# Token tiles of a hybrid encoder's projection placed as runs of rows inside the levels of a delta-rule scan

## The reference

```
proj = x @ w_in                                   # (256, 1024) x (1024, P_IN)
pg, pr, pm = split(proj)
# gMLP: u, v = gelu(pg); v = norm(v) * g + b; y = ws @ v (positions of a chunk of 128) + bs; out = u * y
# RWKV-7, 6 heads x 64, two directions, per step:
sa = state @ a; state = state * w + outer(sa, b) + outer(v, k); out_t = state @ r
# matrix memory (mLSTM), 6 heads x 64, two directions, chunks of 128:
#   gates = pm's last 24 columns -> sums, maxima; scores q k^T weighted by exp(...); num / den; head norm; sigmoid(o)
mix = concat(groups) @ w_out
x = layer_norm(alpha * x + mix)
x = layer_norm(alpha * x + top4_of_32_experts(x))
```

## Time and profile before

| | |
|---|---|
| runs | 1183.06, 1183.63, 1185.85 us, median 1183.63 |
| the profiled execution | span 1184.3 us; the page gives it no other time |
| PE busy | 1132.2 us (96%), 5708 matmuls |
| DVE, ACT, POOL busy | 284.8, 221.9, 33.7 us |
| granted TensorE clock | 0.997 on the mean |
| DMA | 430.95 MB, queue 1 busy 86.2% |
| chain that ended last | PE 73%, DMA 21%, ACT 3%, DVE 2% |

### The profile page before, as it was taken

The page is one execution under the profiler, slowest core; times in us unless marked ns, Lnnn a source line. Parts: engine busy times, 40 slices in busy tenths (PEclk is TensorE's granted clock), DMA queues, the critical chain, the costliest instruction groups (busy, mean ns, idle before and its releaser), DMA issues.

```text
span 1184.3 us, 14440 instructions
## 1 busy us (share of the span) xinstructions
PE 1132.2 (96%) x5708; PEld 493.9 (42%) x5708; DVE 284.8 (24%) x738; ACT 221.9 (19%) x519; POOL 33.7 (3%) x70
## 2 busy tenths in 40 slices
PE   7999999999999999999999999999999999999997
PEld 6875778753333333333333333333333333333332
DVE  1368666662111111111111111111111111111112
ACT  1245655412111111111111111111111111111102
POOL 1000222100000000000000000000000000000000
PEclk9999999999999999999999999999999999999999
DMA  8525202599999999999999999999999999999995
GB/s 336 196 81 198 108 1 78 195 343 390 428 427 429 427 427 428 427 428 428 429 428 427 429 428 429 428 428 429 429 429 428 428 429 429 428 428 428 429 423 217
DMA packets 35649, 430.95 MB, mean 364 GB/s; under 512 B 4086, under 2 KB 4262, under 8 KB 8860
## 3 DMA queue, kind: packets, MB, share of 16 engines
q1 hardware_dynamic: 34364, 428.27, 86.2%
q0 software_dynamic: 528, 1.02, 0.3%
q10 hardware_dynamic: 720, 1.15, 0.3%
HBM read 429.37 MB, written 1.06 MB: 363 GB/s over the span
## 4 chain that ended last, share of the span: by engine, by line
PE 73%; DMA 21%; ACT 3%; DVE 2%; issue 1%; POOLq 0%; SPq 0%; POOL 0%; ACTq 0%; DVEq 0%
PE bank L1484 25%; PE bank L1503 16%; DMA ring<-in_exp_w 14%; DMA pool<-in_exp_w 7%; PE bank L1063 5%; PE bank L1456 4%; PE bank L1440 4%; PE bank L1073 3%; PE bank L1363 2%; PE bank L1468 2%; PE bank L1535 2%; ACT pool L967 1%; PE bank L1238 1%; PE bank L1253 1%; PE bank L1245 1%; PE bank L1528 1%
## 5 line engine op out<-in xcount | busy, mean ns | idle before, releaser
L1484 PE MATMUL bank<-ring,pool 128*64 128x512 f32 x1200 | 265.4, 593 | 10.9 <-DMA ring<-in_exp_w 10.9
L1484 PE MATMUL bank<-pool 128*64 128x512 f32 x848 | 188.4, 594 | 7.1 <-DMA pool<-in_exp_w 7.1
L1484 PEld LDWEIGHTS bank<-ring,pool 128*64 128x64 f32 x1200 | 85.2, 137 | 186.5 <-issue 162.4
L1503 PE MATMUL bank<-ring,pool 128*64 128x512 f32 x620 | 137.7, 595 | 3.8 <-ACT pool L967 3.8
L2191 DVE TENSOR_SCALAR pool<-pool 128x128 f32<-128x128 f32 x64 | 19.4, 346 | 474.1 <-PE bank L1484 474.1
L1484 PEld LDWEIGHTS bank<-pool 128*64 128x64 f32 x848 | 59.9, 137 | 130.6 <-issue 115.2
L942 ACT ACTIVATE pool<-pool 128x512 f32<-128x512 f32 x32 | 20.2, 631 | 416.8 <-DVE pool L2203 416.8
L1503 PE MATMUL bank<-pool 128*64 128x512 f32 x404 | 90.1, 595 | 2.7 <-ACT pool L967 2.7
L2203 DVE TENSOR_SCALAR pool<-bank 128x512 f32<-128x512 f32 x32 | 22.2, 693 | 258.1 <-PE bank L1484 258.1
L1503 PEld LDWEIGHTS bank<-ring,pool 128*64 128x64 f32 x620 | 42.9, 137 | 85.0 <-issue 77.6
L1063 PE MATMUL bank<-pool,ring 128*128 128x256 f32 x272 | 62.1, 391 | 7.0 <-DMA ring<-in_w_in_C 7.0
(11 more groups left out here) (311 smaller groups left out, 903.1 us busy)
## 6 DMA issues: line engine op xcount, KB each, us to landing
ring<-in_exp_w SPq DMA_DIRECT2D x110, 2048.0 KB, 31.9
pool<-in_exp_w SPq DMA_DIRECT2D x73, 2048.0 KB, 34.7
pool<-in_exp_w SPq DMA_DIRECT2D x9, 1024.0 KB, 8.1
ring<-in_exp_w SPq DMA_DIRECT2D x6, 1024.0 KB, 38.4
ring<-in_w_out SPq DMA_DIRECT2D x2, 2048.0 KB, 7.6
ring<-in_w_in_A SPq DMA_DIRECT2D x1, 2048.0 KB, 13.3
ring<-in_w_in_B SPq DMA_DIRECT2D x1, 2048.0 KB, 7.7
ring<-in_w_in_D SPq DMA_DIRECT2D x1, 2048.0 KB, 13.4
```

Of the source, the lines that this page charges most:

```text
L1484: last = mm(bank[4 + g][hp, :], lhs, row(k % 2)[:, o:o + 512], start=False, stop=(k == KD - 1), skip_group_check=(k < 2))
L1503: last = mm(bank[b][SLOTS * hf:SLOTS * hf + SLOTS, :], hidden[:, k % 4, SLOTS * (k // 4):SLOTS * (k // 4) + SLOTS], w[:, 512 * hf:512 * hf ...
```

## The change

1. **Order of the projection.** PE starts the scan of pair 0 right after the 17 transposed tiles. The six token tiles go in as runs of rows (`tok_rows`), at two places of a level: place 0 ahead of its updates, place 1 behind them. The table `FILL` says which rows (tile, first, last) go where, by (pair, level, place); level NL is the pair's last step. Their order is now G, H, F.
2. **Operands.** Pair 0's are made before the scan, between the last projection tiles. Those of pairs 1 and 2 are made by DVE between the levels of pair 0. They are computed in place, so the separate buffers go.
3. **Matrix memory.** Pair 0 has no heads of it any more; pairs 1 and 2 have three each (heads 3pt-3 to 3pt-1). The gate rows are worked out in pair 0, all six are broadcast through DRAM, and the two matmuls that broadcast row 0 go.
4. **ACT.** The token tiles are copied out raw; gelu and the sigmoids of the output gates run once over the whole tensor, with a table change before and after, at the start of pairs 1 and 2, and the sigmoid for the convolution at the start of pair 0.
5. **DMA.** Pieces G and H move to other slots and are issued 2 tiles earlier and right after the 17th tile; x is loaded after pair 0's levels, the output weights in pair 1.

The core of the diff:

```diff
-          "E": (M0 + 512, 256, 0), "F": (M0 + 768, 384, 1), "G": (M0 + 1152, 408, 0), "H": (0, 512, 1)}
+          "E": (M0 + 512, 256, 0), "F": (M0 + 768, 384, 1), "G": (M0 + 1152, 408, 5), "H": (0, 512, 0)}
-TOK_TILES = [(p, c) for p in "FGH" for c in range(NCH)]
+TOK_TILES = [(p, c) for p in "GHF" for c in range(NCH)]
+TOK_BANK = (3, 7, 3, 7, 7, 7)
+FILL = {(0, 1, 0): ((0, 0, 3),), (0, 1, 1): ((0, 3, 6),), (0, 2, 0): ((0, 6, 8), (1, 0, 1)), (0, 2, 1): ((1, 1, 4),),
...
# SP
+            sp.wait_ge(s_proj, NT - 2)
+            load_piece("G")
             sp.wait_ge(s_proj, NT)
-            load_piece("G")
-            sp.wait_ge(s_proj, NT + 2)
             load_piece("H")
...
+            sp.wait_ge(s_proj, NT + 2)
+            sp.dma_start(rowb.rearrange("p h d t -> p (h d t)"), row_bc(rows_d.rearrange("h n -> (h n)"))).then_inc(s_mb, 16)
+            sp.wait_ge(s_a, 12)
+            sp.dma_start(x_tok, x_d).then_inc(s_late, 16)
+            sp.wait_ge(s_vtr, 2)
+            sp.wait_ge(s_ops, NP)
+            load(0, 0, 0)
...
# ACT, before the scans
             z_sigmoids(1)
+            key_scales(0)
             base_of(11)
             base_of(12)
             z_sigmoids(2)
             nc.scalar.preload_act_table_set("natural_log_exp_and_others")
-            base_of(13)
-            base_of(14)
+            decay_exps(0)
...
             A(kk, kk, ACT.Exp, scale=-0.5).then_inc(s_kkd, 1)
+            base_of(13)
+            base_of(14)
...
# ACT, in the levels
             identities()
+            silus()
...
+                    if pt == 0:
+                        if n == 1:
+                            key_scales(1)
+                            decay_exps(1)
+                        if n == 2:
+                            out_gates(0)
+                        if n == 3:
+                            out_gates(1)
+                        if n == 4:
+                            key_scales(2)
+                        if n == 5:
+                            row_exps()
+                        if n == 6:
+                            gate_inputs(2)
+                            decay_exps(2)
+                    else:
+                        if n == 1:
+                            if pt > 1:
+                                args(first)
+                        if n == 2:
+                            if pt == 1:
+                                token_values(4)
+                                act.wait_ge(s_gcol, 1)
+                                A(emt, emt, ACT.Exp, scale=-1.0).then_inc(s_gcev, 1)
+                            factors(first)
+                        if n == 4:
+                            if pt == 1:
+                                token_values(5)
+                            inv_root("g" if pt == 1 else "m")
+                            args(first + 1)
+                        if n == 5:
+                            inv_root("r")
+                            factors(first + 1)
...
+                if pt == 0:
+                    gelus()
+                if pt == 1:
+                    out_sigmoids()
+            inv_root("m")
# PE
+            def tok_rows(j, k0, k1):
+                p, c = TOK_TILES[j]
+                if k0 == 0:
+                    piece_ready(p)
+                    if j < 2:
+                        pe.wait_ge(s_nqe, 3 + j)
+                    else:
+                        pe.wait_ge(s_base, NT + (j - 1 if j < 4 else j))
+                        pe.wait_ge(s_grow, 1)
...
+            pe.wait_ge(s_shift, NT)
             pe.wait_ge(s_vev, 2)
-            pe.wait_ge(s_grow, 1)
-            pe.wait_ge(s_qk, 1)
...
+                    if n == 2 and pt:
+                        scores(3 * pt - 3)
+                    if n == 5 and pt:
+                        scores(3 * pt - 2)
+                    token_work(pt, n, 0)
                     for d in range(2):
                         update(n, d)
+                    if n == 3 and pt == 0:
+                        gate_rows()
+                    if n == 5 and pt:
+                        weigh(3 * pt - 3)
+                    token_work(pt, n, 1)
...
# DVE, before the scans
+            prep_scan(0)
+            prep_relative(0)
             shifted(11)
             shifted(12)
...
+            prep_keys(0)
+            shifted(13)
+            dve.wait_ge(s_kkd, 1)
+            link(V.tensor_tensor(kk, kk, kkraw, ALU.mult))
+            prep_operands(0)
+            shifted(14)
+            shifted(15)
+            prep_scan(1)
+            prep_relative(1)
+            shifted(16)
...
# DVE, in the levels
+                    if pt == 0:
+                        if n == 1:
+                            silu_products()
+                        if n == 2:
+                            prep_keys(1)
+                        if n == 3:
+                            prep_operands(1)
+                        if n == 4:
+                            gate_biases()
+                            prep_scan(2)
+                            prep_relative(2)
+                        if n == 5:
+                            gate_sums()
+                            prep_keys(2)
+                        if n == 6:
+                            gate_maxima()
...
+                        if n == 6:
+                            divide(0)
+                            weights(1)
+                            args(2)
...
+            norm_b("m", flat(hm(1)), HD)
+            mlstm_out(1)
             divide(2 * NP - 1)
```

More of the change, by code:

```diff
@@ L246, in encoder_kernel @@
         mp = rview(2, 2048, 2, 2, 4, P)
-        m_early = [view(o_xT + 512 * b, 2, 2, P) for b in range(4)]
+        m_early = ([view(o_xtok + 512 * b, 2, 2, P) for b in range(4)], [rview(4, 2048 + 512 * b, 2, 2, P) for b in range(4)],
+                   [view(o, 2, 2, P) for o in (o_kT, o_bon)])
         ym = rview(3, 0, 2, 4, P)
@@ L465, in encoder_kernel @@
         s_mrow = sem("m_rows_in_dram")
-        s_mb = [sem(f"m_rows{i}_broadcast") for i in range(2)]
+        s_mb = sem("m_rows_broadcast")
         s_arg = sem("decay_args_ready")
@@ L820, in _, with row_exps @@
[L820 to L825 removed]
+                A(gel[:, j - 2], bank[TOK_BANK[j]][:, 0:512], ACT.Copy).then_inc(s_base, 1)
+            def row_exps():
+                act.wait_ge(s_grow, 1)
+                A(row1[0:6], row1[0:6], ACT.Exp, scale=-1.0).then_inc(s_ach, 1)
+                achain[0] += 1
+                act.wait_ge(s_ach, achain[0])
+                A(row1[0:6], row1[0:6], ACT.Ln, bias=1.0).then_inc(s_gact, 1)
@@ L886, in _ @@
                         A(wbuf[:, d, c::2], pview(4 * d, 0, 2, HD), ACT.Copy).then_inc(s_wev, 1)
-                    if step == 0:
-                        factors(2 * pt + 1)
+                    if step == 0 and pt:
+                        factors(first + 2)
                     for d in range(2):
@@ L1875, in _ @@
-            dve.wait_ge(s_gtr, 1)
-            dve.wait_ge(s_qk, 1)
-            r0, r1, r2, r3 = row0[0:RH], row1[0:RH], row2[0:RH], row3[0:RH]
-            for d in range(2):
-                V.tensor_scalar(r3[:, d], bank[4][0:RH, S * d:S * d + S], gbias[0:RH, d:d + 1], None, ALU.add)
-                last = V.tensor_scalar(r0[:, d], bank[5][0:RH, S * d:S * d + S], gbias[0:RH, 2 + d:3 + d], None, ALU.add)
-            link(last)
-            V.scalar_tensor_tensor(r1, r0, -1.0, r0, ALU.mult, ALU.max).then_inc(s_grow, 1)
+            for i in range(NR):
+                shifted(i)
@@ new lines, in _ @@
+            dve.wait_ge(s_shift, NR)
+            for j in range(NP):
+                last = V.tensor_scalar(kkraw[:, j], kT[:, j], par("kk", j), None, ALU.mult)
+            link(last)
+            V.tensor_tensor(kksq, kkraw, kkraw, ALU.mult).then_inc(s_sq, 1)
+            dve.wait_ge(s_cst, 16)
+            prep_scan(0)
+            prep_relative(0)
+            shifted(11)
+            shifted(12)
+            dve.wait_ge(s_ss, 1)
+            kkf = kk.rearrange("p a s -> p (a s)")
+            V.tensor_scalar(kkf[:, 0:512], bank[6][:, :], 1e-24, None, ALU.max).then_inc(s_kmx, 1)
@@ new lines, in _, with gate_biases @@
+            r0, r1, r2, r3 = row0[0:RH], row1[0:RH], row2[0:RH], row3[0:RH]
+            def gate_biases():
+                dve.wait_ge(s_gtr, 1)
+                dve.wait_ge(s_qk, 1)
+                dve.wait_ge(s_bon, 2)
+                for d in range(2):
+                    V.tensor_scalar(r3[:, d], bank[3][0:RH, S * d:S * d + S], gbias[0:RH, d:d + 1], None, ALU.add)
+                    last = V.tensor_scalar(r0[:, d], bank[7][0:RH, S * d:S * d + S], gbias[0:RH, 2 + d:3 + d], None, ALU.add)
+                link(last)
+                V.scalar_tensor_tensor(r1, r0, -1.0, r0, ALU.mult, ALU.max).then_inc(s_grow, 1)
@@ L2062, in _ @@
+                if pt == 0:
+                    prep_operands(2)
+                else:
+                    if pt == 2:
+                        norm_mean("m", flat(hm(1)), HD)
```

(6 more changed lines are left out.)

455 lines of the change are left out of this document (213 added, 242 removed).

## The result

Nine executions of the changed kernel took 1190.12 to 1200.78 us, median 1190.64, against 1183.63 before (nine executions, 1182.83 to 1186.45): +7.0 us, a ratio of 1.008 with a 95% interval of 1.0057 to 1.0102. The forecast was +3.0. Executions of one kernel are far apart here, and each lists its mean granted clock with its time: 1190.12 to 1190.64 came with 0.991 to 0.993, 1195.5 and 1195.7 with 0.987 and 0.988, 1197.85 with 0.984, 1200.78 with 0.983. The kernel before has 0.996 to 0.998 in the executions that list it.

A forecast was written before the change was run, and what follows sets the result against it. From 796.8 us the weight stream on DMA bounds the kernel, so pair 2's end sets the time. −34.8 + 18.4 + 14.4 + 4.0 + 1.0 = +3.0, giving 1186.6 us, range 1178.5 to 1193.

The forecast's parts named there:

- start of the scans: PE's first scan product comes at 77.0 us instead of 111.8, by a walk through DVE's work: −34.8.
- pair 0: First pair of the scans: token tiles 0 to 3 come in, some work goes, one wait is new; +18.4, to 57.4 us.
- pair 1: Second pair of the scans: token tiles 4 and 5, one more score and new waits; +14.4 us.
- pair 2: Third pair of the scans: no tokens, but three heads instead of two; +4.0 us.
- tail: After the scans: the fourth head's norm and output wait for a root on ACT; +1.0 us.
- The added waits: PE waits in level 4 of pair 0 (+1.9) and pair 1 (+1.8), and for weighings in pairs 1 and 2 (+1.2 each).
- Rival A: Rows fill the waits as DVE and ACT run ahead: 9.0 us of waits go, −6.0, 1177.6 us; chance 0.25.
- Rival B: DVE's insertions between levels delay the masks in pairs 0 and 2: +6 on the forecast, 1192.6 us; chance 0.14.
- Level 5: In pair 2, a score and a weighing are added: +2.0 us net of the 0.43.
- Level 4: In pair 2, the exponent arguments lose the score that covered them: +0.3 us.
- level 2: In pair 2, the score has to wait for the gated output: +0.7 us.
- Rival C: The weight stream absorbs the scans' shift or starts continuous at the same time, so the end stays at 1183.6 us; chance 0.10.

The follow-up runs named there:

- e9: The changed kernel with 256-column matmuls that nobody reads put where PE stands waiting, no wait removed or shortened; 1185.14 us.
- e1_bank3: The changed kernel with DVE releasing bank 3's two gate rows first, so piece H's first row waits only for them; 1188.54 us.
- e11: Unchanged repeat of e7; 1177.42 us.
- e8: The changed kernel with token rows moved from behind to ahead of the updates of the same level, in seven levels of pairs 0 and 1; 1188.14 us.
- e4: The kernel before with two more ACT table loads ahead of the turning-in of pair 1's level 4; 1185.66 us.
- e6: The changed kernel with four edits: bank 3 released first, first weighings and their divide moved earlier, a root put ahead of ACT's last scan copy; 1179.49 us.
- e7: The kernel of e6 with four token rows moved out of the levels to the starts of pairs 0 and 1; 1179.26 us.
- e2: The changed kernel with two matmuls that nobody reads put into PE's wait in pair 1's level 4; 1197.1 us.
- e5: The changed kernel run once more, unchanged, on another chip; 1195.73 us.
- e3: The changed kernel with pair 1's first weighing moved from level 5 into PE's wait for ACT in level 4; 1189.48 us.

## Why the prediction was wrong

The time lay in the range and the direction was right, but the size was off by 4 us, and most of the measured +7.0 comes from something that the forecast didn't have. The added waits are where they were expected; at full clock they and the other terms come to +0.8, too little to tell from nothing. That the kernel came out measurably slower is the clock's doing, so the forecast direction was partly luck. Term by term, without the lower clock (the new lengths are those of the traces in which the stage had none; pair 0 of after is 58.9 less the 1.7):

| term | forecast | measured |
|---|---|---|
| start of the scans | 77.0 | 75.8 (75.3 to 76.7 in ten other traces with this start) |
| pair 0 | 57.4 | 57.2 (57.2 in `e9` too) |
| pair 1 | 51.8 | 51.8 |
| pair 2 | 42.4 | 41.5 |
| tail | +1.0 | 48.7 against 47.6, +1.1 |
| stretches at 1.2 GHz | no term | +6 on the median |

- **Start.** −36.0 and not −34.8; the last shift ended 1.2 earlier than walked.
- **The added waits.** 1.65 for 1.9 (pair 0, level 4), 1.89 in all for 0.43 + 1.8 (pair 1, level 4), 0.96 and 0.95 for 1.2 (weighings). Pair 1's two are 0.6 shorter than forecast, so its other terms are 0.6 longer, and the hit on 51.8 is partly luck. Rival A, that they vanish, is wrong: they are orders on one engine, as argued.
- **Rival B.** No update in pair 0 waits for a mask; DVE's 5.5 us behind level 4 ended at 109.2, before PE needed it, and `e1_bank3`, where PE came sooner, has no such wait either.
- **Pair 2.** 0.9 too long in the forecast. Level 5 (+1.9 for +2.0) and the last steps (+1.2 for +1.2) came as said. Level 4 is 0.2 shorter than before and not 0.3 longer, although PE now waits 0.99 there for ACT, as that costs no more than the score that left; level 2 is 0.5 longer and not 0.7, level 3 is 0.3 shorter and not 0.2.
- **The stream passes it on.** The loop's first matmul at 266.48 gives a span of 1174.0 (`e11`), at 278.47 one of 1186.2 (`e8`), at 281.36 one of 1188.7 (after): the span less this point is 907.5, 907.7 and 907.3. Rival C is wrong.

These terms sum to 275.0 against 274.2 for the kernel before without its own fall (275.68 less 1.5): +0.8. At 0.998 the changed kernel takes 1184.4 by the line, an estimate, and the kernel before 1182.5 to 1184.3 as measured; `e9_idle_rows`, whose idle rows lengthen no stage, has 1184.0 to 1184.4 there. So the change in itself costs about 1 us, less than the 3.0 forecast, and the rest, about 6 of the measured 7.0, is the clock.

**The step that failed** is the sum itself: it had no term for the clock. Every price was taken from rows with a clock of 1.00, and each wait added was priced at its own length (+1.9, +1.8, +1.2, +1.2). Two things in the rows spoke against it. The tail's 0.97 in the earlier trace rows was a fall to 0.51 for 3.5 us that cost 1.5, and I read past it. And "the median of the runs, 1183.6, is 0.7 below the span" took span and time for the same thing: every execution that lists both has a time 1.75 to 1.96 us above its span, so the profiled one took about 1186.1, 2.5 above the median; the fall accounts for it (1.5 on the spot and about 1 behind, below). The slip didn't change the +3.0, but it hid the fall. Once seen, it prices a wait: PE stood 0.62 us in the router and paid 1.5. What the runs show in place of the missing term is about +6 us on the median: 6.3 us in the first trace of after, 10.6 in the second.

**Why more in the changed kernel.** PE waits more in its scans, 14 us in all against 9, and longer at a time, 1.9 at most against 0.8. The places are the start of pair 0, now beside a table change and ahead of other work on ACT; two added waits of 2 us; two of 1 us ahead of weighings, in a stretch of small matmuls. In the traces the clock fell at the starts of pairs 0 and 1, both level 4s, and both weighings. In the two traces with the kernel before's order it fell in the router, in level 3 of pair 0, and behind the wait that `e4` added.

That these places matter is shown by `e6`, `e7` and `e9`, which remove or fill them and have most of the clock back or all of it. Their number alone doesn't decide: `e8` has more of them and falls less often, and in `e4` the clock also fell behind a stretch with PE shown busy for nine tenths. Which place takes the fall in a given execution, and why it is none in some, stays open; two traces of one program disagree on it.

The Trainium skill (TensorE: Matmul & The Clock Gate, HAM oscillation — how this bites in real kernels) prices a stretch at the lower clock at half its length, and has the gaps between matmuls as its cause. The traces agree on the price, 4.6 for 10.3 us and 1.7 for 3.4. The gaps of that section's rule are longer than any wait here; on that the traces differ, and the measurement decides. The forecast should have had it as a rival.

## What to carry to other kernels

Read the granted clock of every stage before its rows are used as prices, and the spread of the clocks over executions before one profile is compared with a median. Where PE waits in small pieces for other engines, a wait of 1 to 2 us can cost two to more than three times itself, in some executions and not in others: price it as a chance, from several executions, and not from one trace. Useful work moved into the waits pays twice, and even matmuls that nobody reads paid here, 5 us and more, when every larger wait had some; put into one of several they gained nothing.

## What the hardware showed that was not expected

- No wait of PE in the changed kernel's scans was longer than 1.9 us, and the clock fell behind waits of 0.8, 1.1 and 1.4 too. It stayed down longest, 13.7 us each, in the last steps of a pair (`e2`, `e5`), with PE shown busy 13.33 of them in `e5`. Small matmuls (64 of 128 rows, 64 columns) are common there; whether they are the reason wasn't tried.
- A fall in the router costs more than its own 1.5 us: where it was there (before at 268, `e7` at 261) span less the loop's first matmul is 908.6 and 909.1, in the eleven other traces 907.2 to 907.8. Why wasn't tried.
- `e2_busy`: filling one wait of several gained nothing (1197.1); with all the larger ones filled (`e9`, 1185.1) what the clock had cost was back.
- When pair 0 starts may decide whether the clock falls there. Seven traces have the same program up to that place. In the four in which it fell (`e1`, `e3`, `e5`, `e6`), pair 0's first product starts 63.7 to 64.2 us behind the first rise to full speed in the trace's record of the clock; in the three in which it didn't (`e2`, after, `e8`) it starts 64.4 to 64.7 us behind it. No run tested this.
